# Which engine issues the last block's gate pieces, and when, in a hybrid layer with an expert retrieval

## What is computed

```python
    def _chunk(args):
        xc, ec, gc = args
        h = jax.nn.gelu(jnp.einsum('tkd,td->tk', u[ec], xc))
        return jnp.einsum('tk,tkd->td', gc * h, v[ec])
```

## Time and profile before

| | us |
|---|---|
| median of three runs | 2746.78 |
| the three runs | 2740.93, 2749.99, 2746.78 |
| the profiled execution | 2744.94 |
| its span, first to last instruction | 2743.1 |
| TensorE busy | 2502.9 (91%) |
| VectorE busy | 2032.0 (74%) |
| ScalarE busy | 1163.2 (42%) |
| GpSimd busy | 955.7 (35%) |

### The profile page before, as it was taken

The page is one execution under the profiler, slowest core; times in us unless marked ns, Lnnn a source line. Parts: engine busy times, 40 slices in busy tenths (PEclk is TensorE's granted clock), DMA queues, the critical chain, the costliest instruction groups (busy, mean ns, idle before and its releaser), DMA issues.

```text
span 2743.1 us, 44706 instructions
## 1 busy us (share of the span) xinstructions
PE 2502.9 (91%) x16674; PEld 2418.8 (88%) x16674; DVE 2032.0 (74%) x3708; ACT 1163.2 (42%) x1933; POOL 955.7 (35%) x641
## 2 busy tenths in 40 slices
PE   6998998878996999999999899897799959999998
PEld 6978998778996999999988799897799959999997
DVE  3545596699995599999865567778998926777774
ACT  3444543235464343333344454332364724333333
POOL 0012006777776123333011100267776731222200
PEclk8999999999998999999999899999999979999998
DMA  7395359985967999999744434799768588999972
GB/s 303 116 299 177 114 184 341 322 285 124 228 176 188 338 366 389 378 391 380 278 163 129 116 108 164 242 345 302 212 173 223 135 245 315 339 343 343 336 281 78
DMA packets 302676, 683.54 MB, mean 249 GB/s; under 512 B 87280, under 2 KB 218736, under 8 KB 257456
## 3 DMA queue, kind: packets, MB, share of 16 engines
q1 hardware_dynamic: 185856, 479.54, 50.4%
q0 software_dynamic: 83632, 185.11, 21.8%
q10 hardware_dynamic: 33024, 16.78, 2.2%
HBM read 594.31 MB, written 86.64 MB: 248 GB/s over the span
## 4 chain that ended last, share of the span: by engine, by line
PE 48%; DVE 21%; issue 11%; POOL 9%; DMA 8%; ACT 2%; ACTq 1%; DVEq 0%; SPq 0%; POOLq 0%
PE ps L1040 19%; PE ps L835 11%; PE ps L981 10%; POOL gate_scratch L721 7%; DVE u_lo L1671 4%; DMA u_rows_s<-in_u_rows_dram,pick_s 2%; DMA gate_scratch<-scat 2%; DVE u_rows_s L1683 2%; DVE mod_p L1968 2%; DVE acc_s L1927 2%; DVE v_lo L1902 2%; POOL u_rows_s L619 1%; PE ps L857 1%; ACTq L1323 1%; DVE w L1911 1%
## 5 line engine op out<-in xcount | busy, mean ns | idle before, releaser
L981 PE MATMUL ps<-h_lo,u_hi 128*128 128x320 f32 x2048 | 656.1, 320 | 158.9 <-DVE u_lo L1671 157.0
L1040 PE MATMUL ps<-w_hi,v_lo 128*128 128x320 f32 (+1 forms) x2048 | 639.4, 312 | 17.5 <-DVE v_lo L1902 17.5
L981 PE MATMUL ps<-h_hi,u_hi 128*128 128x320 f32 x2048 | 641.2, 313 | 0.0
L981 PE MATMUL ps<-h_hi,u_lo 128*128 128x320 f32 x2048 | 641.1, 313 | 0.0
L1040 PE MATMUL ps<-w_lo,v_hi 128*128 128x320 f32 x2048 | 633.4, 309 | 0.0
L1040 PE MATMUL ps<-w_hi,v_hi 128*128 128x320 f32 x2048 | 633.4, 309 | 0.0
L721 POOL DMA_INDIRECT gate_scratch<-scat x256 | 508.2, 1985 | 172.7 <-issue 100.4
L981 PEld LDWEIGHTS ps<-h_lo,u_hi 128*128 128x128 f32 x2048 | 392.6, 192 | 186.3 <-DVE u_lo L1671 179.5
L1333 ACT CAST v_hi<-wring 128x1024 fp32r<-128x1024 f32 x256 | 268.7, 1050 | 506.6 <-PE ps L1040 505.7
L1671 DVE TENSOR_TENSOR u_lo<-wring,u_hi 128x1024 fp32r<-128x1024 f32 x256 | 312.4, 1220 | 175.7 <-ACT u_hi L1258 172.6
L1902 DVE TENSOR_TENSOR v_lo<-wring,v_hi 128x1024 fp32r<-128x1024 f32 x256 | 312.9, 1222 | 159.5 <-ACT v_hi L1333 159.5
(11 more groups left out here) (271 smaller groups left out, 3502.8 us busy)
## 6 DMA issues: line engine op xcount, KB each, us to landing
wring<-in_u_t_dram SPq DMA_DIRECT2D x128, 1024.0 KB, 5.7
wring<-in_v_t_dram SPq DMA_DIRECT2D x128, 1024.0 KB, 7.5
act_scratch<-act_h SPq DMA_DIRECT2D x256, 160.0 KB, 5.8
gate<-gate_scratch SPq DMA_DIRECT2D x64, 640.0 KB, 8.3
act<-act_scratch SPq DMA_DIRECT2D x64, 640.0 KB, 10.3
wring<-in_w_ada_dram SPq DMA_DIRECT2D x24, 1024.0 KB, 5.9
mod_w<-in_w_mod_dram POOLq DMA_DIRECT2D x24, 1024.0 KB, 8.4
wring<-in_w_in_dram SPq DMA_DIRECT2D x20, 1024.0 KB, 5.0
```

The source lines that it names most:

```text
L981: last = nc.tensor.matmul(ps[:, 6 + s % 2, 0:TD], u[:, s % 2, k], hx[:, k, 0:TD], start=(k == 0 and n == 0), stop=(k == KC - 1 and n == 2))
L1040: last = nc.tensor.matmul(ps[:, half * (KC // 2) + c, cols], v[:, of % 4, d], w[:, group * G + of, cols], start=(opening and k == 0), stop ...
```

## The change

ScalarE's eight issues are gone. SyncE issues the same eight writes, with the same regions and semaphores: pieces 0, 1 and 2 among the last hidden units, each before or between the first loads of v, pieces 3 and 4 behind group_loads(2, 0), and 5, 6 and 7 behind group_loads(3, 1). The wait for piece 7 stays where it was, directly behind, and so do GpSimd's waits. Group 0's gates are now loaded behind piece 2, group 1's behind one more tile of v and one more store of activations.

```diff
-            for n in range(WR + 1):
-
-                if n < WR:
-                    sp.wait_ge(ulo_rdy.sem, ulo_rdy.at(l, NB + 2 * (n + 1 - WR)))
-                    load_v(n // 2, n % 2, n)
-                if n:
-                    store_acts(NB // (2 * WR), n)
-                if n == 1:
-                    for sig in g_st[:2]:
-                        sp.wait_ge(sig.sem, sig.at(l, 16 * GT))
...
-                    load_ga(0, 0)
-                    sp.wait_ge(g_st[2].sem, g_st[2].at(l, 16 * GT))
-                    sp.sem_inc(sp_passed.sem, 1)
-                    load_ga(1, 1)
+            def first_v(n):
+
+                sp.wait_ge(ulo_rdy.sem, ulo_rdy.at(l, NB + 2 * (n + 1 - WR)))
+                load_v(n // 2, n % 2, n)
+
+            gates_made(TB - 1)
+            store_gates(TB - 1, 0)
+            first_v(0)
+            store_acts(NB // (2 * WR), 1)
+            store_gates(TB - 1, 1)
+            first_v(1)
+            store_acts(NB // (2 * WR), 2)
+            store_gates(TB - 1, 2)
...
+            load_ga(0, 0)
+            first_v(2)
+            store_acts(NB // (2 * WR), 3)
+            sp.wait_ge(g_st[2].sem, g_st[2].at(l, 16 * GT))
+            sp.sem_inc(sp_passed.sem, 1)
+            load_ga(1, 1)
+            first_v(3)
+            store_acts(NB // (2 * WR), 4)
...
             for n in range(2):
                 group_loads(2 + n, n)
+                for piece in ((3, 4), (5, 6, 7))[n]:
+                    store_gates(TB - 1, piece)
             for sig in g_st[3:]:
                 sp.wait_ge(sig.sem, sig.at(l, 16 * GT))
                 sp.sem_inc(sp_passed.sem, 1)
...
-                if tb + 1 == TB:
-                    act.wait_ge(tq_evac.sem, tq_evac.at(l, NQ))
-                    act.wait_ge(gq_evac.sem, gq_evac.at(l, NQ))
-                    for piece in range(PIECES):
-                        keys = slice(piece * (NK // PIECES), (piece + 1) * (NK // PIECES))
-                        act.dma_start(gate_dram[keys, :, ORDER[tb] * P:(ORDER[tb] + 1) * P].rearrange("a b t -> b a t"), g_all[:, keys]) \
-                            .then_inc(g_st[piece].sem, 16)
```

More of the change, by code:

```diff
@@ L560, in load_v @@
                 sp.dma_start(wring[:, slot].rearrange("p k n -> p (k n)"), v_t[l, g, half]).then_inc(w_ld[slot].sem, 16)
-            for n in range(WR + 1):
-                if n < WR:
-                    sp.wait_ge(ulo_rdy.sem, ulo_rdy.at(l, NB + 2 * (n + 1 - WR)))
-                    load_v(n // 2, n % 2, n)
-                if n:
-                    store_acts(NB // (2 * WR), n)
-                if n == 1:
-                    for sig in g_st[:2]:
-                        sp.wait_ge(sig.sem, sig.at(l, 16 * GT))
-                        sp.sem_inc(sp_passed.sem, 1)
-                    for sig in act_st:
-                        sp.wait_ge(sig.sem, sig.at(l, 16 * (4 * G // AR)))
-                        sp.sem_inc(sp_passed.sem, 1)
-                    sp.wait_ge(sc_st.sem, sc_st.at(l, 16 * 2 * PICKS2))
-                    sp.sem_inc(sp_passed.sem, 1)
-                    load_ga(0, 0)
-                    sp.wait_ge(g_st[2].sem, g_st[2].at(l, 16 * GT))
-                    sp.sem_inc(sp_passed.sem, 1)
-                    load_ga(1, 1)
+            def first_v(n):
[9 more added lines that the diff above has]
+            store_gates(TB - 1, 2)
+            for sig in act_st:
+                sp.wait_ge(sig.sem, sig.at(l, 16 * (4 * G // AR)))
+                sp.sem_inc(sp_passed.sem, 1)
+            sp.wait_ge(sc_st.sem, sc_st.at(l, 16 * 2 * PICKS2))
+            sp.sem_inc(sp_passed.sem, 1)
+            for sig in g_st[:2]:
+                sp.wait_ge(sig.sem, sig.at(l, 16 * GT))
+                sp.sem_inc(sp_passed.sem, 1)
+            load_ga(0, 0)
+            first_v(2)
+            store_acts(NB // (2 * WR), 3)
+            sp.wait_ge(g_st[2].sem, g_st[2].at(l, 16 * GT))
+            sp.sem_inc(sp_passed.sem, 1)
+            load_ga(1, 1)
+            first_v(3)
+            store_acts(NB // (2 * WR), 4)
             def group_loads(g, n, ga=True):
```

## The result

The changed kernel took 2764.66 us in the median of 5 runs (2759.93 to 2773.67), the kernel before 2744.12 us (5 runs, 2740.93 to 2749.99): a ratio of 1.0077, 95% interval 1.0051 to 1.0102. It is slower by 20.5 us in the medians, 0.8%, where 12.5 were forecast. The profiled execution is the slowest of the five, 2773.67 us with a span of 2771.9, 28.8 more than the span before.

The account below looks back on a forecast made before the run. The prediction took ScalarE's eight gate issues as first limit at the change of stages, the scatter-adds close under them. Its terms, -10.7 + 2.4 - 1.5 + 12.8 + 6.7 + 2.8 = +12.5, gave 2757.4 us, range 2738 to 2770.

Parts of the forecast that it names:

- the forecast's own case: Whole kernel: slower, mainly by stalls at group 4, 2757.4 us, range 2753 to 2763; chance 0.42.
- third rival: "Bound by transfers": layer 1's second stage loses 19 us to five pieces, plus late mod_w and row loads; 2763 to 2773; chance 0.12.
- adds end earlier, layer 1: Change of stages: last batch's hole shrinks from 4.44 to 0.30 us, adds land at 883.9; gain 6.0 us (4.4 to 7.4).
- adds end earlier, layer 2: Change of stages: gain 4.0 us from the hole and 0.7 from a quicker last landing, 4.7 (3 to 8).
- gate loads of groups 0 and 1, layers 1 and 2: Start of second stage: group 1's load comes late, loss 1.2 us per layer; group 0's load is covered.
- group 2's load in layer 1: Second stage: GpSimd's c_b and mod_w loads come later, so this load is alone; gain 1.5 us.
- stall at group 4, layer 1: Second stage: SyncE waits for piece 7 before group 4's loads, act lands at 977.9; loss 12.8 us.
- stall at group 4, layer 2: Second stage: act issued at 2308.4 behind the pieces, landing in 7.8 to 10.0 us; loss 6.7 us.
- clock, layers 1 and 2: After each stall at group 4: the clock falls and first matmuls run slower; loss 1.4 us per layer.
- No stall: Second rival, at group 4: pieces land before TensorE needs group 4; 2735 us, or 2732 to 2737; chance 0.13.
- ScalarE goes on at once: Fourth rival, change of stages: idle of some 27 us in each layer goes; near 2690 us; chance 0.03.
- Same path with quick loads: First rival: group 4 lands in 7.8 us in layer 1 too, clock hardly falls; 2747 us (2741 to 2753); chance 0.30.

Follow-up runs that it names:

- e2_late_wait: Changed kernel with SyncE's wait for pieces 3 to 7 moved from ahead of group 4 to ahead of group 12: 2764.91 us, ratio 1.0075 to the kernel before.
- e5_both_late: e2_late_wait with GpSimd's wait also split (pieces 0-2 before sel and v rows, 3-4 before c_b, 5-7 before mod_w): 2757.80 us, ratio 1.0057 to the kernel before.
- e7_adds_alone: Changed kernel with SyncE waiting for the end of the scatter-adds before it issues piece 0: 2763.26 us in one execution.
- e9_best_order: e5_both_late with pieces 3-7 one behind each of groups 2-6, piece 0 after the adds, group 0 before second V load, later c_b/mod_w: 2745.27 us, ratio 1.0002.
- e10_no_late_pieces: e9_best_order without storing pieces 3 to 7 of the last block: 2776.21 us, not comparable as a whole; read by its second stages alone.
- e3_after_fewer_adds: Changed kernel with 112 of its 128 scatter-adds in each layer: 2716.85 us in one execution.
- e4_before_fewer_adds: Kernel before the change with 112 of its 128 scatter-adds in each layer: 2744.36 us in one execution.
- e6_pool_only: Changed kernel with only GpSimd's wait split as in e5_both_late, SyncE still waiting for all pieces ahead of group 4: 2769.48 us in one execution.
- e8_spread: e5_both_late with pieces 5 and 6 behind group 3's loads, piece 7 behind group 4's, c_b and mod_w seven units later: 2752.44 us, ratio 1.0026.

## Why the prediction was right, and where it was not

The direction, the range and the main mechanism held. The size did not: 20.5 us against 12.5, and by the medians 2764.66 lies above the forecast's own case (2753 to 2763) and within the third rival's. All the large errors below go the same way. One of the prediction's own signs of being wrong came true in layer 1: TensorE's idle time there stayed near 27, 26.7 us where 19 to 23 were forecast. By the terms of the sum:

| term | predicted | measured in the profiled execution |
|---|---|---|
| adds end earlier, layer 1 | -6.0 | +0.4 at the restart |
| adds end earlier, layer 2 | -4.7 | -4.4 |
| gate loads of groups 0 and 1, layers 1 and 2 | +1.2, +1.2 | +3.2, +3.0 |
| group 2's load in layer 1 | -1.5 | -1.5 |
| stall at group 4, layer 1 | +12.8 | +12.4 |
| stall at group 4, layer 2 | +6.7 | +5.5 |
| clock, layers 1 and 2 | +1.4, +1.4 | +2.6, +4.2 |

**Group 4** is right, and in layer 1 by its own steps: the second V load at 945.4 forecast and about 947.1 measured, pieces at an end at 961.5 and landed at 963.84, act issued at 963.0 and 965.05, landing 14.92 and 14.36. In layer 2 two errors partly cancel: act is issued 74.8 us after the restart and not 69.8, 3 of the 5 since the whole stage is that late by then, and it lands in 6.4 us and not in 7.8 to 10.0. The price was right, but a sentence beside it was too simple: that the expert rows land "behind the same wait"; and of c_b, released with them, the prediction priced only what it does to group 4's landing. They are a second limit, and e2_late_wait shows it: take SyncE's wait away and c_b costs 11 of the 12 us. And below both waits lies the one that e5_both_late shows, the time for which three pieces hold SyncE's queue.

**The adds in layer 1** are the step that failed: "Afterwards only piece 0 is in flight there, so I take the hole as a normal 0.30". The hole is not made by the pieces alone. It is 1.83 to 1.97 us with nothing in flight beside it (e7_adds_alone, e9_best_order) and 2.53 with piece 0, in this layer. And piece 0 sits in the gap ahead of the batch, where I had looked for no cost: 6.27 us against 2.53. The prediction also took the batch's start of the old trace, 865.83, for the new one, where it is 872.01. Of these 6.2 us, 3.7 are the longer gap, and 2.5 were there a batch earlier (846.35 against 843.83), before any piece was issued. Gap and hole together were 6.7 us before, 8.8 in the change, and 4.4 without any piece. The size of the gain was right for a kernel that the change isn't: with the adds alone the idle time falls by 4.3 and 7.3 us, 11.6 in all, against the 10.7 forecast. That the two are so close is luck in part: the hole was put 1.5 to 1.7 us too short, and the last landing, 3.6 us behind the end of the last add, was 1.4 in the change and in e7_adds_alone.

**Groups 0 and 1** were mis-sized: 1.2 per layer, 3.2 and 3.0 measured. The 1.2 was for group 1 alone, near the low end of its bounds (0.7 to 4); group 0's load, called covered, was not. Its act was issued at 909.36 and VectorE waited 2.12 us for it, until 917.73; TensorE lost 1.71. Group 1's cost 2.18, where a wait of 0.74 us stood before.

**The clock**: behind each stall of group 4 TensorE, which had stood, runs at the lower level, 1.2 GHz (0.50 granted), before it is at 2.4 GHz again: 23 matmuls in 6.11 us from 981.59 to 987.70, and 18 in 4.94 us from 2337.86 to 2342.80, 0.27 us each where the pace is 0.147. The forecast had one slow start for each stall, priced by nine matmuls; more than nine ran at the lower level. Over the whole second stages TensorE's busy time for the same matmuls grew by 2.6 us in layer 1 (417.2 to 419.8) and 4.2 in layer 2, where the rows are, before and after:

```profile
2238.57:2743.00 504.43, 490.37 (x3308) 488.00 (x3308) 344.88 (x356) 189.06 (x217) 89.51 (x67) 0.98 0.79 290
```

```profile
2254.46:2771.80 517.34, 494.58 (x3308) 491.47 (x3308) 344.74 (x356) 189.22 (x217) 86.10 (x67) 0.97 0.81 296
```

Sum of the terms measured: 0.4 - 4.4 + 6.2 - 1.5 + 12.4 + 5.5 + 6.8 = 25.4, of a span that is 28.8 longer; 3.2 are the part between the stages, and 0.2 are not placed. The medians differ by 20.5, less than this execution. The stages of the three kernels with the change's placement of pieces 1 to 7 (change, e2_late_wait, e7_adds_alone) are longer than before by 30 to 34 us in all; so the adds must give back some 10 to 13 us on average. The table shows most of it: with one piece beside them the idle time is 24.7 to 26.7 us in seven layers and 16.6 to 18.9 in three, 23.2 in the mean of ten; with eight it is 26.9 in the mean of the five layers seen. Twice the difference is 7.4, which leaves 25 of 32, against 20.5 in the medians; the rest is open. The profiled execution had none of the three short ones.

**The rivals.** "No stall" and "ScalarE goes on at once" are out. "Same path with quick loads" is out in layer 1 (14.4 us) and right in layer 2, where the stall is 5.5. Its "clock hardly falls" is out in both (2.6 and 4.2 us). "Bound by transfers" named a mechanism that the runs bear out: GpSimd's loads meet loads that are late, and in layer 1, where it stood, one piece behind each group still costs 7.0 us (e9_best_order against e10_no_late_pieces). It is no bound on the stage of layer 2, which carries all five pieces without a wait when they are two groups apart. That spacing was not tried in layer 1.

## What to carry to other kernels

Where an engine waits for several things, the chain names only the last: before you take that one away, read how far under it the next lies, because that is all that you will gain unless the change makes the next one faster too. Read it by when the next one has landed, not by when it was issued: here the last add was issued 5 us before ScalarE was free, but landed only 1.1 us before it in layer 1, and after it in layer 2. Moving transfers from a stretch in which TensorE stands still into one that keeps the DMA engines busy was a loss here until they were spread so thin that each was caught up before the next; five pieces in bursts of two and three, with the later first loads, made layer 2's stage 12.9 us longer, and no wait was left there when one went out every second group. In layer 1, where the pieces' memory is wanted for other work, only the kernels that send pieces 3 to 7 out early keep the stage at 429 to 432 us; there a transfer that releases memory belongs early even though its readers come late.

## What the runs showed of the hardware

Scatter-adds, 128 cells to an instruction and eight instructions to a batch, are issued 1.85 us apart by GpSimd in the last batch, but its fifth waits 1.8 to 2.0 us even when no piece is in flight, where I had expected 0.30. That hole stands at the 125th add of every layer with 128, and the last batch of the kernels with 112 has none (e3_after_fewer_adds, e4_before_fewer_adds); its cause stays open. Beside piece 0 it was 1.9 to 2.5 us (5.7 once, in e5_both_late, where the piece went out within the batch), beside five or eight pieces 4.3 to 5.8. The wait for the batch before is 2.2 to 2.9 us with nothing beside it and 4.9 to 6.3 with piece 0 in flight. The last add lands 2.9 to 3.1 us after its start with no piece or one, 3.1 with five (one layer), and 5.3 to 6.8 with eight. With none beside them the idle time was 22.1 to 22.7 us in all eight layers seen; with one piece it varied from 16.6 to 26.7, with eight from 18.6 to 33.4. In the layers with none or one whose last batch starts after the gates' end (the end of ScalarE's last copy into g_all), the idle time is close to 17.2 us plus the distance of that start from it: 1.5 us gave 18.7 (e6_pool_only, layer 2), 4.9 and 5.2 gave 22.1 and 22.3 (e7_adds_alone), 7.7 and 8.6 gave 25.0 and 25.8. Five kernels have the same code up to this place in layer 1 (the change, e2_late_wait, e5_both_late, e6_pool_only, e8_spread), and there the last batch starts 8.9, 7.6, -4.4, 8.6 and 8.6 us after the gates' end. So where in the batches the gates happen to end moves the kernel by several microseconds from run to run, as much as most of the edits tried here.

Three pieces of 1 MB took 10.9 us to issue when GpSimd was held, 16.3 when it loaded beside them, and a piece with none ahead of it 0.4: in these runs the time that an issue blocks its engine goes with what else is on the DMA engines. "DMA: Bandwidth & Descriptors" of the Trainium skill (section "Issuing engines are not separate DMA queues") has all queues share the same 16 DMA engines; the 10.9 and 16.3 us agree with it.
